# GpSimd adds the squares of 20 norms, and TensorE sums over partitions with two matmuls in place of eight

## What is computed

```python
def rmsnorm(x, g):
    xf = x.astype(jnp.float32)
    y = xf * lax.rsqrt(jnp.mean(xf * xf, axis=-1, keepdims=True) + EPS)
    return (y * g.astype(jnp.float32)).astype(x.dtype)

for i in range(DEPTH):
    u = rmsnorm(x, g_mix[i])
    y = pool_mixer(u, ...) if i % 2 == 0 else conv_mixer(u, ...)
    x = x + y
    x = x + mem_attend(rmsnorm(x, g_attn[i]), mem_k[i], mem_v[i], w_q[i], w_o[i])
    x = x + sq_relu_mlp(rmsnorm(x, g_ffn[i]), w_up[i], w_down[i])
return rmsnorm(x, g_final)
```

## Time and profile before

| | |
|---|---|
| median of three runs | 1645.23 us |
| the profiled execution | 1645.83 us |
| span of its slowest core (core 7) | 1644.3 us |
| spans of the eight cores | 1633.1 to 1644.3 us |
| TensorE matmul busy | 1597.1 us, 97% |
| VectorE busy | 879.7 us, 54% |
| ScalarE busy | 511.9 us, 31% |
| GpSimd busy | 80.4 us, 5% |

### The profile page before, as it was taken

The page is one execution under the profiler, slowest core; times in us unless marked ns, Lnnn a source line. Parts: engine busy times, 40 slices in busy tenths (PEclk is TensorE's granted clock), DMA queues, the critical chain, the costliest instruction groups (busy, mean ns, idle before and its releaser), DMA issues.

```text
span 1644.3 us, 27615 instructions; the slowest of 8 cores (1633.1 to 1644.3 us)
## 1 busy us (share of the span) xinstructions
PE 1597.1 (97%) x9500; PEld 915.7 (56%) x9500; DVE 879.7 (54%) x1987; ACT 511.9 (31%) x988; POOL 80.4 (5%) x117
## 2 busy tenths in 40 slices
PE   6899998999999999999999999999999999999997
PEld 5664554555555555555555555555555555555565
DVE  5746676554443444456666564676744444444455
ACT  4755642221221221223222135553321121111244
POOL 0010120000000000000000000121100000000000
PEclk9999999999999999999999999999999999999999
DMA  9995997437307345124000067699405303203013
GB/s 256 188 204 117 205 211 154 74 49 106 59 7 124 62 64 75 29 30 74 1 0 1 1 103 135 155 200 227 108 14 99 56 1 52 52 1 52 16 70 124
DMA packets 70388, 146.20 MB, mean 89 GB/s; under 512 B 4414, under 2 KB 22078, under 8 KB 70236
## 3 DMA queue, kind: packets, MB, share of 16 engines
q0 software_dynamic: 47184, 76.21, 31.2%
q1 hardware_dynamic: 23068, 68.23, 13.5%
HBM read 207.18 MB, written 14.42 MB: 135 GB/s over the span
## 4 chain that ended last, share of the span: by engine, by line
PE 90%; DVE 3%; DMA 3%; ACT 2%; issue 1%; DVEq 0%; ACTq 0%; SPq 0%; POOL 0%; POOLq 0%
PE PS L284 87%; DVE MEM L313 2%; PE PS L288 2%; DMA MEM<-cv 1%; PE PS L293 1%; DMA MEM<-ck 1%; ACT MEM L301 1%; ACT MEM L304 1%; DMA mn<-MEM 1%; DVE MEM L337 0%; DVE MEM L317 0%; DVE MEM L331 0%; DMA MEM<-gv 0%; ACT MEM L329 0%; ACT PS L301 0%
## 5 line engine op out<-in xcount | busy, mean ns | idle before, releaser
L284 PE MATMUL PS<-MEM 128*128 128x416 bf16 (+3 forms) x8588 | 1526.4, 340 | 25.5 <-DVE MEM L317 9.0
L284 PEld LDWEIGHTS PS<-MEM 128*128 128x128 bf16 (+1 forms) x8588 | 843.1, 99 | 696.7 <-issue 44.0
L317 DVE TENSOR_TENSOR MEM<-PS,MEM 128x416 f32<-128x416 f32 (+5 forms) x601 | 339.4, 584 | 336.5 <-PE PS L284 279.5
L301 ACT ACTIVATE MEM<-PS 128x416 f32<-128x416 f32 (+3 forms) x465 | 233.9, 515 | 627.7 <-PE PS L284 526.9
L317 DVE TENSOR_TENSOR MEM<-MEM 128x416 bf16<-128x416 f32 (+1 forms) x320 | 186.6, 588 | 257.3 <-ACT MEM L301 257.3
L313 DVE SCALAR_TENSOR_TENSOR MEM<-MEM 128x416 bf16<-128x416 f32 (+5 forms) x314 | 191.7, 659 | 89.7 <-ACT MEM L301 84.6
L301 ACT ACTIVATE MEM<-MEM 128x1 f32<-128x1 f32 (+7 forms) x201 | 125.5, 633 | 107.7 <-DVE MEM L317 84.9
L337 DVE SCALAR_TENSOR_TENSOR MEM<-MEM 128x256 f32<-128x256 f32 x256 | 91.7, 421 | 15.0 <-DMA MEM<-ck 14.9
L329 ACT COPY MEM<-PS 128x416 f32<-128x416 f32 (+4 forms) x68 | 36.8, 543 | 178.7 <-PE PS L284 158.8
L329 ACT CAST MEM<-PS 128x416 bf16<-128x416 f32 (+3 forms) x101 | 52.0, 516 | 69.3 <-PE PS L284 53.7
L301 ACT ACTIVATE PS<-PS 128x416 f32<-128x416 f32 (+2 forms) x65 | 33.0, 507 | 99.6 <-PE PS L284 99.6
(11 more groups left out here) (26 smaller groups left out, 81.9 us busy)
## 6 DMA issues: line engine op xcount, KB each, us to landing
MEM<-ck SPq DMA_DIRECT2D x64, 512.0 KB, 7.9
MEM<-w_up POOLq DMA_DIRECT2D x8, 2048.0 KB, 18.3
MEM<-cv POOLq DMA_DIRECT2D x64, 256.0 KB, 8.4
MEM<-w_down POOLq DMA_DIRECT2D x6, 2048.0 KB, 16.2
MEM<-x SPq DMA_DIRECT2D x16, 512.0 KB, 11.4
MEM<-w_kv POOLq DMA_DIRECT2D x4, 2048.0 KB, 27.7
MEM<-qd SPq DMA_DIRECT2D x32, 256.0 KB, 8.3
y<-MEM SPq DMA_DIRECT2D x15, 512.0 KB, 2.6
```

The source lines that it names most:

```text
L284: P.add(PE, "c", lambda e, o=out.ap, l=lhsT.ap, r=rhs.ap: e.matmul(out=o, lhsT=l, rhs=r, start=start, stop=stop), [lhsT, rhs], [out])
L301: P.add(ACT, "c", lambda e, o=out.ap, i=in_.ap: e.activation(out=o, in_=i, func=func, bias=bias, scale=sc), rd, [out])
L317: P.add(eng, "c", lambda e, o=out.ap, a=in0.ap, b=in1.ap: e.tensor_tensor(out=o, in0=a, in1=b, op=op), [in0, in1], [out])
```

## The change

For 20 of the norms a new function `norm_sum` follows each half of the squares. GpSimd adds the chunks one after another in fp32, with RSTD as the running sum: three adds behind the first half, four behind the second. Then it casts the sum to bf16 into chunk 0 of SQ, and writes what the cast left out (sum minus cast) into chunk 1. TensorE multiplies these two chunks by ones, where it multiplied eight. Five norms keep the eight matmuls (`summed=False`, and the one in mixer 0): the first of mixer 0, tile 4's attention norm and tile 4's MLP norm in each layer.

The squares are also placed earlier in some loops, and two norms later: in the convolution mixer at channels 2 and 4 (3 and 5 before), for tile 0 at the end of it behind groups 0 and 1 of `p2` (3 and 5); tile 2's MLP norm with squares at O groups 0 and 1 (2 and 4) and the norm at 7 (6); tile 3's with squares behind groups 0 and 1 (0 and 2) and the norm behind 7 (5); those of tiles 0 and 1 of the convolution mixer with squares one MLP item earlier. The attention loop over k is as it was, but for the sums.

```diff
--- before.py
+++ after.py
@@ -408,10 +408,20 @@
     def norm_a(c0, n, SQ):
         act(SQ(sl(0, NCH), sl(0, n)), X(sl(0, NCH), sl(c0, c0 + n)), AF.Square)
 
-    def norm_b(c0, n, grow, outv, SQ, RSTD, extra=None, defer=None):
+    def norm_sum(n, half, SQ, RSTD):
+        s = RSTD(sl(0, n))
+        for c in range(half * 4, half * 4 + 4):
+            if c:
+                tt(s, SQ(0, sl(0, n)) if c == 1 else s, SQ(c, sl(0, n)), ALU.add, eng=POOL)
+        if half:
+            cp(SQ(0, sl(0, n)), s, eng=POOL)
+            tt(SQ(1, sl(0, n)), s, SQ(0, sl(0, n)), ALU.subtract, eng=POOL)
+
+    def norm_b(c0, n, grow, outv, SQ, RSTD, extra=None, defer=None, summed=True):
         bk = nxt()
-        for c in range(NCH):
-            mm(PSv(bk, 0, n), ONESB(), SQ(c, sl(0, n)), c == 0, c == NCH - 1)
+        nk = 2 if summed else NCH
+        for c in range(nk):
+            mm(PSv(bk, 0, n), ONESB(), SQ(c, sl(0, n)), c == 0, c == nk - 1)
         act(PSv(bk, 0, n), PSv(bk, 0, n), AF.Ln, scale=1.0 / D, bias=EPS)
         act(RSTD(sl(0, n)), PSv(bk, 0, n), AF.Exp, scale=-0.5)
         for c in range(NCH):
@@ -422,10 +432,6 @@
                 defer.append(f)
         if extra is not None:
             extra(RSTD)
-
-    def norm(c0, n, grow, outv, SQ, RSTD, extra=None):
-        norm_a(c0, n, SQ)
-        norm_b(c0, n, grow, outv, SQ, RSTD, extra)
 
     def kv_units(l, MEMN, ST, after_k, after_v, SV=None, late=None):
         SV = SV or ST
@@ -750,6 +756,7 @@
             c0, n, npmt, ns = TILES[ti]
             h = sl(half * 4, half * 4 + 4)
             act(self.SQ(h, sl(0, n)), X(h, sl(c0, c0 + n)), AF.Square)
+            norm_sum(n, half, self.SQ, self.RSTD)
 
         def nb(self, ti, grow=R_MIX + 1):
             c0, n, npmt, ns = TILES[ti]
@@ -817,7 +824,7 @@
                 for c in range(NCH):
                     if ti == 0 or c > 0:
                         self.p1(ti, c)
-                    if ti + 2 < NT and c in (3, 5):
+                    if ti + 2 < NT and c in (2, 4):
                         self.na(ti + 2, c // 4)
                     if ti + 2 < NT and c == 7:
                         self.nb(ti + 2)
@@ -826,8 +833,8 @@
                     wrelease("cin_h")
                 for c in range(NCH):
                     self.p2(ti, c)
-                    if ti == NT - 1 and c in (3, 5):
-                        self.na(0, c // 4)
+                    if ti == NT - 1 and c in (0, 1):
+                        self.na(0, c)
                     if ti == NT - 1 and c == 7:
                         self.nb(0, R_ATTN + 1)
                 if ti == NT - 1:
@@ -864,13 +871,15 @@
         for i in range(2):
             memset(PZ[i](), 0.0, eng=POOL)
 
-        def norm_h(ti, half):
+        def norm_h(ti, half, summed=True):
             c0, n, npmt, ns = TILES[ti]
             act(SQ(sl(half * 4, half * 4 + 4), sl(0, n)), X(sl(half * 4, half * 4 + 4), sl(c0, c0 + n)), AF.Square)
-
-        def norm_t(ti, grow, defer=None):
+            if summed:
+                norm_sum(n, half, SQ, RSTD)
+
+        def norm_t(ti, grow, defer=None, summed=True):
             c0, n, npmt, ns = TILES[ti]
-            norm_b(c0, n, grow, lambda c, c0=c0, n=n: U3(c, sl(c0, c0 + n)), SQ, RSTD, defer=defer)
+            norm_b(c0, n, grow, lambda c, c0=c0, n=n: U3(c, sl(c0, c0 + n)), SQ, RSTD, defer=defer, summed=summed)
 
         def Qgroup(k, ec):
             ti = seq[k]
@@ -998,11 +1007,11 @@
         for i in range(3):
             SDK(i)
         for half in range(2):
-            norm_h(seq[1], half)
+            norm_h(seq[1], half, False)
         for ec in range(NCH):
             Qgroup(0, ec)
             if ec == 3:
-                norm_t(seq[1], R_ATTN + l)
+                norm_t(seq[1], R_ATTN + l, summed=False)
         slots = [(0, 3), (1, 0), (1, 2), (1, 3), (2, 1), (2, 2), (2, 3), (3, 1), (3, 2), (3, 3), (4, 1), (4, 2)]
         late_n = []
         for k in range(5):
@@ -1040,11 +1049,11 @@
                 wspread_step(2)
         for ec in range(NCH):
             Ogroup(seq[4], ec)
-            if ec in (2, 4):
-                norm_h(2, ec // 2 - 1)
+            if ec in (0, 1):
+                norm_h(2, ec)
             if ec == 3:
                 slot()
-            if ec == 6:
+            if ec == 7:
                 norm_t(2, R_FFN + l)
         wspread_step(NCH)
 
@@ -1146,20 +1155,20 @@
         def endB(ec):
             if ec == 0:
                 Ogroup(4, 6)
-                norm_h(4, 0)
+                norm_h(4, 0, False)
                 Ogroup(4, 7)
                 wrelease(f"wo{l}")
             if ec == 2:
-                norm_h(4, 1)
+                norm_h(4, 1, False)
             if ec == 4:
-                norm_t(4, R_FFN + l)
+                norm_t(4, R_FFN + l, summed=False)
 
         def n3_hook(ti):
             def f(ec):
-                if ec in (0, 2):
-                    norm_h(ti, ec // 2)
+                if ec in (0, 1):
+                    norm_h(ti, ec)
                 mid(ec)
-                if ec == 5:
+                if ec == 7:
                     norm_t(ti, R_FFN + l)
             return f
 
@@ -1203,9 +1212,10 @@
             for _ in kv1[0]:
                 pass
             conv.state()
+        if j in (15, 17):
+            for half in range(2):
+                conv.na((j - 15) // 2, half)
         if j in (16, 18):
-            for half in range(2):
-                conv.na((j - 16) // 2, half)
             conv.nb((j - 16) // 2)
 
     layer(0, side0, tail0)
```

## The result

The changed kernel took 1661.17 us in the median of four runs (1658.35 to 1663.01), the kernel before 1644.59 us beside it (1643.72 to 1646.36): a ratio of 1.0102, with a 95% interval of 1.0083 to 1.012, or +16.6 us. Slower was forecast, with 1649.5 us (+4.2 in its own sum) and a range of 1632 to 1663. The sign and the range held; the size was four times too small. The time stands nearest to the third rival's, 1659.0.

The account below looks back on a forecast made before the run. TensorE, busy for 97% of the span, was taken to bound the kernel, VectorE and transfers parts of the attention. Sum: -21.0 + 2.1 + 3.0 + 5.3 + 0.3 + 3.4 + 11.1 = +4.2, so 1649.5 us, range 1632 to 1663.

Parts of the forecast that it names:

- the third rival: GpSimd and VectorE each block the other wholly: 20.7 us in place of 11.1, time 1659.0 us, chance 0.25.
- The price of an operation: On GpSimd: an add 1.07 us, the cast 0.63, all nine operations of a norm 9.3.
- Tile 0's norm: At the end of the convolution mixer: 4.0 us available, 9.3 needed, so 5.3 us late.
- The three inner norms: Inside the convolution mixer: each 1.0 us late, 3.0 in all, and 1.0 each more from meeting VectorE's tap multiplies.
- The clock: Half clock after stops in the mixer: 3.4 us behind the 5.3 us stop and 1.7 behind one other.
- Matmuls saved: Six fewer in each of 20 norms, 120 at 0.175 us: 21.0 us, or 1.05 us a norm.
- What the attention takes back: Two norms' saving, one a layer, lost to waits for transfers: 2.1 us (1 to 5).
- Tile 3's MLP norm: In the first MLP products: covered without contention, 10.0 us against 9.3; with five waits 1.1 us late each, 2.2.
- Tile 2's MLP norm: Called tile 2's FFN norm: its squares move ahead of the matmuls, so it was said to fit, at no cost.
- Contention: VectorE slowed beside GpSimd's adds: 11.1 us with its clock loss, a little over half of the upper end, 20.7.
- The queue: Weight and cv transfers issued behind sums in GpSimd's queue: nothing taken (0 to 2 us).
- The full-blocking rival: Each engine waits for the other's whole instruction, with 4.0 us where VectorE drives ck transfers: 1659.0 us, chance 0.25.

Follow-up runs that it names:

- x1: The changed kernel without any of GpSimd's sums, so 20 norms multiply only two chunks of squares; 1630.43 us, ratio 0.991 to the kernel before.
- x7: The changed kernel with the running sum of tile 2's MLP norm in buffer RD in place of RSTD; 1668.02 us, ratio 1.0105.
- x2: The changed kernel with GpSimd's adds, subtract and cast replaced by memsets that read nothing, with the same waits; 1667.43 us, ratio 1.0138.
- x10: The changed kernel with the first two samples' cv transfers issued ahead of the first attention sum; three runs at 1656.48 to 1656.91 us, ratio 1.0094 over one more.
- x8: x5 with tile 1's attention norm in each layer also summed; 1646.7 us, ratio 0.9987.
- x9: x8 with the first two samples' cv transfers issued ahead of that norm's sum; 1634.5 us, ratio 0.9937.
- x5: The changed kernel without sums in the attention loops' norms and tile 2's MLP norm, and the mixer's squares earlier; 1642.8 us, ratio 0.9949.
- x6: x5 with tile 2's MLP norm of each layer also summed, its running sum in buffer RD; 1642.0 us, ratio 0.9954.

## Why the prediction was right in sign and wrong in size

By its own steps; the three parts of its sum are put together for the table. The sign came from the mixer, which held. In the attention the sign itself was wrong, -6.0 against +8.8, and those 14.8 us are more than the whole error (the other parts take back 2.7); the range held it because it had been drawn wide enough for the third rival.

| | predicted | measured |
|---|---|---|
| mixer, 4 norms: -4.2 + 3.0 + 5.3 + 3.0 + 5.1 (clock) | +12.2 | +11.8 |
| MLPs, 4 norms: -4.2 + 2.2 | -2.0 | -4.3 |
| attention, 12 norms: -12.6 + 2.1 + 0.3 + 4.2 | -6.0 | +8.8 |
| sum | +4.2 | +16.3 |

- **The price of an operation** held: 1.1 us start to start for 1.07, cast 0.56 for 0.63, all nine 9.4 for 9.3 (970.13 to 979.56). The Trainium skill's factor of 1.96 (GPSIMD Engine Reference, 3.1, Elementwise) gave an estimate of 1.16 us, a little above the 0.99 measured for one and the 1.1 from start to start.
- **The mixer** held in each term. Tile 0's norm: 5.3 predicted, 5.2 measured, for the chain of nine operations against 3.9 us available. The three inner norms: 2.0 each with contention; measured 1.55 + 0.78, 1.51 + 0.67 and 1.14 + 0.76. The clock: 5.1 predicted; behind these stops TensorE's granted clock is at its half level (1.2 GHz) for 3.4 us near 778 and 6.8 near 978, half of which is 5.1 (that is the slowest core; in the median core it is 6.8 us in all, so 3.4).
- **Matmuls saved**: 0.175 us each, as x1's mixer and MLPs show. What the attention takes back was under: 4.3 (x1), not 2.1.
- **Tile 3's MLP norm** was in time in both layers (1.1 late each predicted). Tile 2's MLP norm, which lies at the end of the attention and was predicted to fit, was not: 1.51 + 0.78 and 1.42 + 0.67. I had priced its squares by ScalarE and had not asked where the sum is kept. RSTD is still read by the norm before, which holds the first add back by 5.2 us (259.45 for 254.25). x7 shows that this wait covered a second cause, the meeting with VectorE's multiplies, which costs more than it.
- **Contention** was the largest open term, and I chose "a little over half" between its ends. Its mechanism is the upper end: a product beside an add takes 1.14 to 1.18 us, 0.42 and the add's remainder. That agrees with the rule of the Trainium skill (SBUF — State Buffer, Who interferes with whom) that one of the two waits for all of the other; x2 agrees with its other half, that a GpSimd instruction that only writes does not meet VectorE's second input. I should have given the full price, and not a mean of two mechanisms, of which only one can be true. Where it falls was wrong too: not on the multiplies of 133.7 to 138, because the first add waits for them (RSTD again: the Square ends at 134.72, the adds begin at 137.70), but on the products behind them. 2.1 us a layer at that place was about right (x10: 5.47 less 3.3). Two more meetings that TensorE waits for were left out: tile 2's last operations with the next slot's products (the stop of 1.87 us), and tile 3's norm, called covered, whose first adds meet three products at 171 us (the stop of 1.32).
- **The queue** was priced at "nothing (0 to 2)", with the reason that a late cv is not needed for 14 us. The reason holds for cv and misses who shares the DMA engines: 1 MB sent later collides with the 32 KB that the chain does wait for. x8 against x9: 0.0050 of the time by their ratios, 8.2 us for two layers (each ratio is uncertain by 2.5 us), and 7.4 us by part, with nothing else changed in the kernel, though on two chips; TensorE's idle alone is 2.7 and 3.0 us more in the two layers. In the changed kernel its share is smaller, since q's wait overlaps the products': there x10 shows 4.5 us by part in the attention and about 5 in the whole time. Of the steps that had bounds this is the one that measured outside them.
- **The clock in the attention** was not priced. TensorE's time at half level is 10.2 us in each layer in the median core (5.1 and 3.4 before), up to 6 us of loss in both together, half of the difference: the idle grew from 3.5 to 6.2 us, and others were added. This loss is inside the shares of contention and of the queue, not beside them.

Together in the attention: x1 keeps 8.3 of the matmuls' 12.6 us, and against x1 the sums cost 7.0 + 10.1 = 17.1 us. x2, with the queue's delay and without contention, stands 4.2 + 4.6 = 8.8 above x1 and 8.3 under the changed kernel. So about half of those 17 us is contention and half is late transfers and other waits for GpSimd; with x2's four cores 7 us apart the halves are known to some 3 us. How the second half divides is open beyond the first transfers (the longer waits for ck at 231 and 1127 us have no experiment), because mending one uncovers another, as x7 and x10 show.

The full-blocking rival had the total nearly right (1659.0), and its mechanism is shown. But it needed its 4.0 us "where VectorE drives the ck transfers" to reach 20.7 us of contention; the queue, which is in none of the rivals, has part of what it put there. That its total came out so near is partly luck.

## What to carry to other kernels

Work moved to an idle engine is free only if three things hold: nothing waits for the end of its chain, the engines whose reads it shares are not on the path beside it, and no transfer stands behind it in that engine's queue. Check the third for who else uses the DMA engines at the later moment, and not only for who needs the late data. Ten of the twenty norms met all three once the mixer's squares and the first cv transfers were placed earlier, and moving those alone gave 0.6% where all twenty cost 1.0%. Removing a wait is worth something only if what comes earlier by it does not meet something else: the free buffer for tile 2's sum made TensorE's stop longer.

## What had not been expected of the hardware

- A small transfer is delayed by larger ones of another queue: 32 KB took 1.6 us until it could be read when no cv transfer was issued just ahead of it (x5, x9), and 4.8 to 5.4 on the first four cores of x8, with 1 MB of cv issued 3 us ahead.
- A running sum in a buffer that another engine still reads delayed the chain by 3.0 and 5.2 us (changed kernel, 137.70 for 134.72 and 259.45 for 254.25), which no duration of an operation shows.
- A VectorE product (0.42 us) beside GpSimd's adds takes 1.18 us, also when several follow one another: the two alternate (x10), and eight multiplies pay 0.72 us for each of three adds (4.58 to 6.73 us). GpSimd's three adds in turn take 3.73 in place of 3.2 us there (x6). With writes only on GpSimd nothing of this is left (x2).
